# A hybrid decoder layer on one core: the transposed half of a block-wise triangular inverse, two chunks in one product at three of its levels

## The reference, cut to what matters

```python
kbeta = kc * bc[..., None]
a_mat = jnp.where(strict, jnp.einsum('bhnid,bhnjd->bhnij', kbeta, kc) * decay, 0.0)
t_mat = lax.linalg.triangular_solve(a_mat + eye, jnp.broadcast_to(eye, a_mat.shape),
                                    left_side=True, lower=True)
u = jnp.einsum('bhnij,bhnje->bhnie', t_mat, vc * bc[..., None])
w = jnp.einsum('bhnij,bhnjd->bhnid', t_mat, kbeta * jnp.exp(gcum)[..., None])
```

## Time and profile before

| | |
|---|---|
| median of 3 runs | 1237.97 us (1237.43 to 1241.09) |
| profiled execution | 1239.19 us, of which the span of its instructions is 1237.4 |
| PE matmul busy | 1209.7 us, 8814 instructions |
| VectorE, ScalarE, GpSimd busy | 797.1, 517.8, 301.3 us |
| chain that ended last | PE 83%, VectorE 9%, ScalarE 4% |
| PE clock granted, mean | 0.994 of full |

### The profile page before, as it was taken

The page is one execution under the profiler, slowest core; times in us unless marked ns, Lnnn a source line. Parts: engine busy times, 40 slices in busy tenths (PEclk is TensorE's granted clock), DMA queues, the critical chain, the costliest instruction groups (busy, mean ns, idle before and its releaser), DMA issues.

```text
span 1237.4 us, 25567 instructions
## 1 busy us (share of the span) xinstructions
PE 1209.7 (98%) x8814; PEld 1129.0 (91%) x8814; DVE 797.1 (64%) x1948; ACT 517.8 (42%) x1375; POOL 301.3 (24%) x275
## 2 busy tenths in 40 slices
PE   5999999999999999999999999999999999999997
PEld 4999999999999999999999999999999999999996
DVE  7476477657765776577657765776567658465544
ACT  6343334533453345334533453345334536531211
POOL 1114121411141114112411241123112322322211
PEclk8999999999999999999999999999999999999998
DMA  7332453245324532453245324532443266323253
GB/s 248 93 94 63 140 165 103 63 139 165 103 62 139 165 103 62 139 165 103 62 140 164 103 63 142 161 103 63 146 157 103 88 202 195 94 85 98 73 204 139
DMA packets 79646, 151.56 MB, mean 122 GB/s; under 512 B 12353, under 2 KB 22242, under 8 KB 77986
## 3 DMA queue, kind: packets, MB, share of 16 engines
q1 hardware_dynamic: 78254, 148.78, 38.5%
q10 hardware_dynamic: 1312, 1.59, 0.5%
HBM read 132.20 MB, written 17.27 MB: 121 GB/s over the span
## 4 chain that ended last, share of the span: by engine, by line
PE 83%; DVE 9%; ACT 4%; issue 3%; DMA 1%; DVEq 0%; SPq 0%; ACTq 0%
PE PJ L600 17%; PE PJ L596 11%; PE PJ L597 11%; PE PJ L598 11%; PE PJ L601 8%; PE MX L803 3%; DVE memx L1556 2%; PE MX L784 2%; PE MX L795 1%; PE PJ L916 1%; PE MX L727 1%; PE MX L707 1%; PE PJ L917 1%; PE PJ L918 1%; PE MD L855 1%
## 5 line engine op out<-in xcount | busy, mean ns | idle before, releaser
L600 PE MATMUL PJ<-h,w_hi 128*128 128x512 f32 x1110 | 416.9, 412 | 0.0
L1932 POOL TENSOR_TENSOR w_lo<-w_raw,w_hi 128x512 fp32r<-128x512 f32 x160 | 216.5, 1354 | 814.3 <-ACT w_hi L986 814.3
L596 PE MATMUL PJ<-h,w_hi 128*128 128x264 f32 (+1 forms) x1248 | 366.4, 294 | 1.2 <-ACT memx L1016 1.2
L597 PE MATMUL PJ<-h,w_hi 128*128 128x264 f32 (+1 forms) x1248 | 354.1, 284 | 0.0
L598 PE MATMUL PJ<-h,w_lo 128*128 128x264 f32 (+1 forms) x1248 | 353.9, 284 | 0.0
L601 PE MATMUL PJ<-h,w_lo 128*128 128x256 f32 x1110 | 310.7, 280 | 0.0
L600 PEld LDWEIGHTS PJ<-h,w_hi 128*128 128x128 f32 x1110 | 209.0, 188 | 43.4 <-DVE w_lo L1361 1.7
L596 PEld LDWEIGHTS PJ<-h,w_hi 128*128 128x128 f32 x1248 | 235.8, 189 | 5.4 <-issue 3.9
L597 PEld LDWEIGHTS PJ<-h,w_hi 128*128 128x128 f32 x1248 | 236.1, 189 | 1.6
L986 ACT ACTIVATE w_hi<-w_raw 128x512 fp32r<-128x512 f32 x320 | 196.6, 624 | 92.9 <-PE PJ L598 82.4
L598 PEld LDWEIGHTS PJ<-h,w_lo 128*128 128x128 f32 x1248 | 234.8, 188 | 0.0
(11 more groups left out here) (326 smaller groups left out, 1818.9 us busy)
## 6 DMA issues: line engine op xcount, KB each, us to landing
w_raw<-in_w_in SPq DMA_DIRECT2D x256, 256.0 KB, 2.7
w_raw<-in_w_out SPq DMA_DIRECT2D x64, 256.0 KB, 2.8
kv<-in_cache_win_k SPq DMA_DIRECT2D x24, 512.0 KB, 4.6
kv<-in_cache_win_v SPq DMA_DIRECT2D x16, 512.0 KB, 4.6
out<-memx SPq DMA_DIRECT2D x16, 260.0 KB, 4.3
mem<-in_x_prompt SPq DMA_DIRECT2D x4, 1024.0 KB, 10.1
S<-in_state_delta SPq DMA_DIRECT2D x8, 512.0 KB, 3.5
out<-S SPq DMA_DIRECT2D x8, 512.0 KB, 2.9
```

The costliest lines, as they stand in the source:

```text
L596: pe.matmul(ps, wh, h_hi[:, k, tok], start=k == 0, stop=False)
L597: pe.matmul(ps, wh, h_lo[:, k, tok], start=False, stop=False)
L600: pe.matmul(both, wh, h2[:, :, k, tok], start=k == 0, stop=False)
L1932: pool.tensor_tensor(w_lo[:, par, 4 * q:4 * q + 4, :], w_raw[:, q, :, :], w_hi[:, par, 4 * q:4 * q + 4, :].bitcast(F32), ALU.subtract).the ...
```

## The change

At levels 3, 4 and 5 the four transposed products become two. The stationary operand of a pair is a new matrix `b_W[:, j]`: the odd rows (in blocks of 2^n) from `b_U[:, j]`, the even ones from `b_U[:, 2 + j]`. ScalarE makes the first part in bank 0 (`masked`), scaling rows by a 0/1 column; VectorE multiplies the other pair by the complement and adds (`both_rows`). The mask for level n + 1 is issued one step behind the Y copy of level n, the multiply-add one step behind the update of level n. The columns come with one more small input, loaded at the start on SP; VectorE's first wait for the tables, and ScalarE's first step of `mix_b`, count it.

```diff
+            sp.dma_start(odd_rows[:].rearrange("p a n -> p (a n)"), c_odd).then_inc(s["s_loaded"], 16)
...
-                    for c in chunks if n < LEVELS - 1 else (2, 3):
-                        last = pe.matmul(blocks(mx(3)[:, c, :], n, c // 2), b_U[:, c, :],
-                                         blocks(b_Y[:, c % 2, :], n, c // 2), start=True, stop=True)
+                    if n in W_LEVELS:
+                        pe.wait_ge(s["mix_W"], len(W_LEVELS) * h + W_LEVELS.index(n) + 1)
+                        for j in range(2):
+                            last = pe.matmul(crossed(mx(3), n, False, j), b_W[:, j, :],
+                                             b_Y[:, j, :].rearrange("p (k a s) -> p a k s", a=2, s=1 << n),
+                                             start=True, stop=True)
+                    else:
+                        for c in chunks if n < LEVELS - 1 else (2, 3):
...
+            def masked(n):
+                act.activation(mx(0)[:, 0:2, :], b_U[:, 0:2, :], ACT.Copy, scale=odd_rows[:, 0, n:n + 1]).then_inc(
+                    s["mix_Y"], 1)
...
                     act.activation(b_Y[:, 0:2, :], mx(1)[:, 0:2, :], ACT.Copy).then_inc(s["mix_Y"], 1)
                     yield
+                    if n + 1 in W_LEVELS:
+                        act.wait_ge(s["mix_UT"], UTS * h + 2 * n - 1)
+                        if n in W_LEVELS:
+                            act.wait_ge(s["mix_W"], len(W_LEVELS) * h + W_LEVELS.index(n) + 1)
+                        masked(n + 1)
...
+            def both_rows(h, n):
+                dve.wait_ge(s["mix_Y"], YS * h + y_count(n) - 1)
+                if n == 1:
+                    dve.wait_ge(s["mix_U0"], 3 * h + 3)
+                else:
+                    dve.wait_ge(s["mix_UT"], UTS * h + 2 * n - 3)
+                dve.scalar_tensor_tensor(b_W[:], b_U[:, 2:4, :], odd_rows[:, 1, n:n + 1], mx(0)[:, 0:2, :], ALU.mult,
+                                         ALU.add).then_inc(s["mix_W"], 1)
...
                 for n in range(1, LEVELS):
                     yield
+                    if n in W_LEVELS:
+                        both_rows(h, n)
                     yield
                     dve.wait_ge(s["mix_Z"], UTS * h + 2 * n)
...
-            dve.wait_ge(s["s_loaded"], 48)
+            dve.wait_ge(s["s_loaded"], 64)
```

More of the change, by code:

```diff
@@ L53, in tables @@
     t["c_levels"] = lev
+    odd = (i[:, None] >> np.arange(LEVELS)[None, :]) % 2
+    t["c_odd"] = np.concatenate([odd, 1 - odd], 1).astype(f)
     row, term = np.arange(4 * NB) % NB, np.arange(4 * NB) // NB
@@ L175, in build @@
 def build(nc, x_prompt, x_sample, cache_k, cache_v, state_conv, state_delta, g_pre, w_in, w_ba, conv_w, a_log, dt_bias,
-          onorm_w, w_out, g_post, c_ident, c_upper, c_causal, c_levels, c_lnmask, c_rope, c_terms,
+          onorm_w, w_out, g_post, c_ident, c_upper, c_causal, c_levels, c_lnmask, c_rope, c_terms, c_odd,
           y_p, y_s, k_new, v_new, c_new, c_old, st_p, st_s):
@@ L252, in build @@
         kvl = sb("kvl", [4 * NB, 2, P])
+        b_W = sb("b_W", [P, 2, P])
+        odd_rows = sb("odd_rows", [P, 2, LEVELS])
         terms = sb("terms", [4 * NB, NB + 2])
@@ L301, in build, with y_count @@
         UTS = 2 * (LEVELS - 1)
+        W_LEVELS = range(3, LEVELS - 1)
+        YS = LEVELS - 1 + len(W_LEVELS)
+        def y_count(n):
+            return n + sum(1 for m in W_LEVELS if m <= n)
         DST = [(xq, 3), (xq, 3), (xq, 3), (xz, 0), (xq, 3), (xk, 0), (xv, 0), (xz, 0)]
@@ L336, in build @@
             "hg_ok mix_T1 mix_ss mix_lnrk mix_rs mix_scal mix_gb mix_tok mix_kbT_ps mix_kbT mix_arg mix_D "
-            "mix_kk mix_qk mix_A mix_QK mix_B mix_U0 mix_T_ps mix_T mix_Y_ps mix_Y mix_Z mix_UT ch_kS ch_r "
+            "mix_kk mix_qk mix_A mix_QK mix_B mix_U0 mix_T_ps mix_T mix_Y_ps mix_Y mix_Z mix_W mix_UT ch_kS ch_r "
             "ch_v_ps ch_v ch_S_ps ch_o_ps ch_S ch_o1 ch_o o_sq on_rs o_n o_T z_sig_b z_ok_b gated_b gB_out S_out "
@@ L787, in mix_b @@
                     yield
-                    pe.wait_ge(s["mix_Y"], (LEVELS - 1) * h + n)
+                    pe.wait_ge(s["mix_Y"], YS * h + y_count(n))
                     if n == 1:
@@ L801, in mix_b @@
                     last.then_inc(s["mix_Z"], 1)
-                    for c in chunks if n < LEVELS - 1 else (2, 3):
-                        last = pe.matmul(blocks(mx(3)[:, c, :], n, c // 2), b_U[:, c, :],
-                                         blocks(b_Y[:, c % 2, :], n, c // 2), start=True, stop=True)
+                    if n in W_LEVELS:
[6 more added lines that the diff above has]
+                        for c in chunks if n < LEVELS - 1 else (2, 3):
+                            last = pe.matmul(blocks(mx(3)[:, c, :], n, c // 2), b_U[:, c, :],
+                                             blocks(b_Y[:, c % 2, :], n, c // 2), start=True, stop=True)
                     last.then_inc(s["mix_Z"], 1)
@@ L1179, in mix_b @@
                     act.wait_ge(s["gated_b"], h)
+                else:
+                    act.wait_ge(s["s_loaded"], 64)
                 for x in (b_U, b_T):
@@ L1197, in mix_b @@
                 yield from idle(8)
+                if 1 in W_LEVELS:
+                    act.wait_ge(s["mix_U0"], 3 * h + 3)
+                    act.wait_ge(s["mix_T"], 2 * h + 2)
+                    masked(1)
                 for n in range(1, LEVELS):
@@ L2037 @@
         "conv_w", "a_log", "dt_bias", "onorm_w", "w_out", "g_post"]
-_CONST = ["c_ident", "c_upper", "c_causal", "c_levels", "c_lnmask", "c_rope", "c_terms"]
+_CONST = ["c_ident", "c_upper", "c_causal", "c_levels", "c_lnmask", "c_rope", "c_terms", "c_odd"]
 _OUTS = [(1, TP, D), (NB, 1, D), (NH, HD, TT), (NH, HD, TT), (NH, 3, HD, CW - 1 + NB), (NB, CW - 2, CONV_CH),
```

## The result

The kernel after takes 1241.2 us (median of 11 runs, 1240.6 to 1241.9); the kernel before, run beside it, 1239.0 (11 runs, 1237.4 to 1241.1). The ratio is 1.0017, 95% interval 1.0009 to 1.0025: slower by 2.2 us, within what I called no change, and outside my range of 1230.5 to 1238.0. The profiled execution took 1241.2, its span 1239.4, 2.0 more than before.

What follows compares the result with a forecast made beforehand. PE's own instruction stream was taken to bound the kernel. Saving 24 x 0.445 = 10.7 us, less waits 7 x (0.44 + 0.05 + 0.50) = 6.9, gains 3.8: 1234.2 us against the median of 1237.97, range 1230.5 to 1238.0.

Steps and rivals of the forecast that it cites:

- three levels of wide products: PE, levels 3 to 5: eight 64-column instructions become four of 128, saving 0.445 us a level, 1.33 a head.
- wait at level 3: PE waits for ScalarE's Y copy, late behind the mask and L1006: 0.44 us in heads 1 to 7.
- wait at level 4: PE waits for the second half of level 3's update on VectorE, L1637: 0.05 us in heads 1 to 7.
- wait at level 5: PE waits for VectorE's multiply-add before the transposed products: 0.50 us in heads 1 to 7.
- head 0: Has no L1261 or L1797, and its rope is queued before level 4's update: keeps all 1.33 us.
- the rope: VectorE's three query-rotation instructions (L1489 to L1491) right after level 4's update, forecast to end at 493.6 under GpSimd's port use.
- Late next is L1749: VectorE after level 5's multiply-add: L1749, then level 5's update, come late; PE needs the update only at next level's Y.
- Level 5's port order: VectorE and GpSimd taking turns: L1489 ends 491.09, L1981 491.6, L1490 492.15, L1996 493.04, L1491 493.6.
- Level 5 eats everything: Rival: GpSimd runs L1981 and L1996 ahead of L1489, PE waits 0.98 us at level 5; 1237.6 us, chance 0.20.
- Columns: Rival: PE's products cost by their columns, so nothing is saved and the waits are paid; 1244.9 us, chance 0.04.
- a dear mask: Rival: ScalarE's mask into PSUM takes 0.8 us or more, making it slower; 1244.5 us at 1.2 us, chance 0.06.
- hidden waits: Rival: cheap mask (0.27 us), L1361 gets the port before L1981, most waits stay hidden; 1230.4 us, chance 0.20.

Runs made afterwards that it cites:

- the kernel with the multiply-add ahead of the rope: The change, with level 5's multiply-add issued right behind level 4's update, ahead of VectorE's query rotation: 1236.1 us against 1239.4 for the kernel before, ratio 0.9979.
- the added work alone: Masks and multiply-adds run, but PE does the narrow products of the kernel before and waits for none of it: 1242.7 us against 1239.3, ratio 1.0035.
- both moves: The change, with the query side (sigmoid) issued ahead of the mask and the query rotation behind level 5's update: 1229.9 us against 1239.4 before, ratio 0.9925.
- the wide products alone: The change without masks, multiply-adds and PE's wait for them, products taking `b_U`, output not the reference's: 1229.5 us against 1239.3 before, ratio 0.9918.

## Why the prediction was wrong

To set head 3 of the two traces on one clock: Y of level 3 loads at 481.25 after and at 482.10 before (a shift of 0.84 us from the heads in front), so 0.84 is added to a time of after. The terms, per head:

| term | predicted, us | measured, us |
|---|---|---|
| three levels of wide products | 1.33 | 0.45 + 0.39 + 0.39 = 1.23 |
| wait at level 3 | 0.44 | 0.44 |
| wait at level 4 | 0.05 | 0.14 |
| wait at level 5 | 0.50 | 1.21 |
| sum, heads 1 to 7 | 0.34 gained | 0.56 lost |
| head 0 | 1.33 gained | 1.23 gained, no wait |

Seven times 0.56, less 1.23, is 2.7 us lost; 2.0 (span) to 2.2 (medians) were measured. The rest is the start of the kernel: the first level of head 0 came 0.55 us earlier in this profile. The extra table, put at nothing, shows no cost there, but the start varies by more than the 0.5 us that it could have cost.

**The step that failed is "Level 5's multiply-add stands behind the rope: where L1749 starts at 493.91 today it starts at 493.86."** I gave it L1749's place. But the first outer-product add is issued in step 43, with the rope, and the multiply-add one step behind level 4's update, in step 44: L1749 stays in front, and its 0.66 us, 0.58 net of overlap, go on top. By the common clock the rope ends at 493.84 instead of the forecast 493.6, the multiply-add starts at 494.68 instead of 493.86, 0.82 late; PE came 0.12 later than I had it (Z at 492.70 + 0.84 = 493.54, 0.28 ahead of before, not 0.40). 0.50 + 0.82 - 0.12 = 1.20, and 1.21 was measured. (Of the 0.82, 0.24 is the later end of the rope and 0.58 L1797. No run took L1797 alone out of the way: its share is read from the order in the trace.) Both step numbers could be read from the code: the term's mechanism was right, what stood in the queue was counted one instruction short. "Late next is L1749" was wrong in the same way, and so was its being harmless: the kernel with the multiply-add ahead of the rope shows PE waiting for that add.

**Level 3 was right to the hundredth.** The mask is 0.479 us long against 0.49 taken, it stands ahead of L1025, L1010 comes late, the Y copy and Z with it. The cure by order (the mask behind L1025) and the added work alone show the same cause from two sides. The Trainium skill's page "ScalarE: Activation LUTs", section "Step-by-step: what each stage is for", says that ScalarE writes PSUM faster than SBUF; here 0.479 into PSUM stands beside 0.492 into SBUF, which agrees but decides nothing.

**Level 4 was right in its chain, small in its size.** L2029 ends at 485.49 on the common clock, L1396 at 486.04, the update's second half at 486.70: the forecast numbers. But PE's load came 0.12 us after that end, not 0.04. (The row of that load names no releaser, only `issue`; Y reads `b_T`, which this half writes.) The Trainium skill's page "SBUF — State Buffer", section "Who interferes with whom", describes the port pair that VectorE and GpSimd share as an exclusive lock, and says that issue order decides who blocks. L1396 agrees: it started at 484.05, 0.06 after L2029, took 1.15 instead of 0.70 and ended 0.55 after L2029.

**Level 5's port order was another than I took,** at little cost. I had the rope's first instruction at the port before GpSimd's masked matrix. But L2029 started at 489.60, right behind L1980, and L1524 at 489.69, 0.09 later; so L1524 had to wait for L2029, L2044 came after it (1.49 instead of 1.03), then L1525, and L1526 had the port to itself: an end 0.24 late. PE, and with it level 4's update and the rope, was 0.12 later than forecast by then; 0.12 earlier, and with GpSimd where it was, L1524 would have been first (an estimate from these starts).

**The products** cost by the instruction: both widths 0.11 us. I had multiplied that by four at every level; where the outer product follows, 0.05 of the saving is lost in front of it.

**The rivals.** "Level 5 eats everything" was the nearest, with 1237.6: right in that level 5's wait of about a microsecond takes the gain, wrong in its mechanism (it gave all that came on top to the port; the rope's later end made 0.24 us of it, L1749 0.58). Columns and a dear mask were refuted; hidden waits happen only with both moves. The rule that I set against the rows for the columns (the Trainium skill, "TensorE: Matmul & The Clock Gate", "Back-to-back issue gap") is given there for an isolated product, not for a stream of loads and products as here, so it spoke for that rival less than I had it; the wide products alone, at a ratio of 0.9918, decide. And the two figures of the dear mask do not come from one count: 0.8 us fits 0.1 and 0.2 us of wait for every 0.1 of mask, 1244.5 fits 0.1 at each of the two levels, by which the line would be crossed at about 1.0 us. Nothing hung on it, since the mask took 0.479.

## What to carry to other kernels

Before costing an instruction put into a hand-ordered queue, write out which instructions stand in front of it and behind it in its step, by the count of steps of every generator in the list, not by what ran near that time in the old trace. On a kernel that one engine fills, work added elsewhere was free where it fell into idle time and was paid for fully where it stood ahead of a late operand: the same 48 instructions gave 1241.2 or 1229.9 us by two changes of order. When a wait is cured by moving one instruction forward, look at what it now stands ahead of: here the wait moved to the next operand (0.53 of 1.21 us remained), while moving the neutral neighbour back left none.

## What was not expected of the hardware

How little decides who gets the port between VectorE and GpSimd. (An instruction's length in the trace holds its wait for the port.) Of two GpSimd instructions without a gap between them, the second let VectorE in before it where VectorE's instruction had started first (L1361 at 483.85, L1981 at 483.97, which then took 1.11 us), and kept it out where it had itself started first (L2029 at 489.60, L1524 at 489.69, which then took 1.13). In both cases the earlier start had the port, by 0.12 and by 0.09 us. And the start of the kernel varies: the first level of head 0 came between 1.1 us earlier and 1.4 us later than before in the profiled executions, a spread larger than the whole result of 2.2 us, so the terms were sized by distances inside a trace.
